# Gated embedding of a two-layer block: four gates by chunk with embedding products between them, table stores moved, tail of the gates interleaved

## What is computed

```python
        h = rmsnorm(x, g_ffn2_pre[i])
        x = x + 0.5 * rmsnorm(swiglu(h, w2_gate[i], w2_up[i], w2_down[i]), g_ffn2_post[i])

        h = rmsnorm(x, g_ple_pre[i])
        e = jax.nn.sigmoid(h @ w_ple_gate[i]) * (p[i].astype(x.dtype) @ w_ple_proj[i])
        x = x + rmsnorm(e, g_ple_post[i])
```

## Time and profile before

| | us |
|---|---|
| median of three runs | 3695.54 |
| their lowest and highest | 3688.07, 3698.82 |
| the profiled execution, its own time | 3689.66 |
| its span, first to last instruction | 3688.4 |
| PE busy in the span | 3459.0 (94%) |
| POOL busy | 2418.4 (66%) |
| DVE busy | 1802.9 (49%) |

### The profile page before, as it was taken

The page is one execution under the profiler, slowest core; times in us unless marked ns, Lnnn a source line. Parts: engine busy times, 40 slices in busy tenths (PEclk is TensorE's granted clock), DMA queues, the critical chain, the costliest instruction groups (busy, mean ns, idle before and its releaser), DMA issues. The chain is left out here.

```text
span 3688.4 us, 42456 instructions
## 1 busy us (share of the span) xinstructions
PE 3459.0 (94%) x15371; PEld 2698.8 (73%) x15384; DVE 1802.9 (49%) x1934; ACT 719.3 (20%) x1404; POOL 2418.4 (66%) x1113
## 2 busy tenths in 40 slices
PE   7999998899998999999899998986999999779998
PEld 6888765688876888775678886654788877558886
DVE  5452535454647545334464474687454323354521
ACT  2110133311123111103321112214311100231100
POOL 7888741488876887763178886650488777328875
PEclk9999998999998999999899999997999999899999
DMA  3233220122331223221022332220122333102232
GB/s 122 97 100 103 86 69 18 58 95 96 109 120 60 94 95 103 86 91 46 18 88 96 104 104 92 92 69 1 56 94 96 103 104 108 40 26 95 97 100 94
DMA packets 84366, 305.98 MB, mean 83 GB/s; under 512 B 9360, under 2 KB 9616, under 8 KB 83856
## 3 DMA queue, kind: packets, MB, share of 16 engines
q1 hardware_dynamic: 80928, 292.59, 23.7%
q10 hardware_dynamic: 3312, 11.71, 0.8%
HBM read 300.07 MB, written 4.19 MB: 82 GB/s over the span
## 5 line engine op out<-in xcount | busy, mean ns | idle before, releaser
L469 POOL TENSOR_TENSOR WH<-raw,zero 128x1024 fp32r<-128x1024 f32 (+1 forms) x554 | 1045.2, 1887 | 1200.6 <-DMA raw<-in_w 1105.7
L471 POOL TENSOR_TENSOR WL<-raw,WH 128x1024 fp32r<-128x1024 f32 (+1 forms) x554 | 1375.0, 2482 | 43.5
L539 PE MATMUL psA<-HH,WH 128*128 128x512 f32 x1216 | 483.6, 398 | 2.3 <-DVE PROJ L1509 2.3
L540 PE MATMUL psA<-HH,WL 128*128 128x512 f32 x1216 | 474.7, 390 | 0.0
L541 PE MATMUL psA<-HL,WH 128*128 128x512 f32 x1216 | 474.7, 390 | 0.0
L541 PE MATMUL psC<-HIDL,WH 128*128 128x512 f32 x1056 | 417.1, 395 | 0.0
L539 PE MATMUL psC<-HIDH,WH 128*128 128x512 f32 x1056 | 417.1, 395 | 0.0
L540 PE MATMUL psC<-HIDH,WL 128*128 128x512 f32 x1056 | 417.1, 395 | 0.0
L1338 DVE TENSOR_TENSOR HIDL<-Y,HIDH 128x512 f32 (+1 forms) x132 | 257.1, 1948 | 126.7 <-ACT HIDH L1060 126.7
L539 PE MATMUL psC<-HH,WH 128*128 128x512 f32 x800 | 314.0, 392 | 3.8 <-DVE HL L1410 3.8
L541 PE MATMUL psC<-HL,WH 128*128 128x512 f32 x800 | 312.3, 390 | 0.0
(11 more groups left out here) (274 smaller groups left out, 4896.2 us busy)
## 6 DMA issues: line engine op xcount, KB each, us to landing
raw<-in_w SPq DMA_DIRECT2D x554, 512.0 KB, 3.3
X<-in_x ACTq DMA_DIRECT2D x4, 512.0 KB, 8.9
NRAW<-in_mem ACTq DMA_DIRECT2D x2, 1024.0 KB, 5.2
out<-Y SPq DMA_DIRECT2D x8, 256.0 KB, 2.1
POSI<-in_pos ACTq DMA_DIRECT2D x4, 256.0 KB, 3.0
PRAW<-in_p ACTq DMA_DIRECT2D x2, 512.0 KB, 4.5
table_F<-newF ACTq DMA_DIRECT2D x2, 512.0 KB, 5.1
table_I<-newI ACTq DMA_DIRECT2D x2, 512.0 KB, 7.8
```

Source lines behind the costliest of these rows:

```text
L469: pool.tensor_tensor(WH[j][:, 0:w], raw[j][:, 0:w], zero[:, 0:1].broadcast_to([P, w]), ALU.subtract).then_inc(w_hi, 1)
L471: pool.tensor_tensor(WL[j][:, 0:w], raw[j][:, 0:w], WH[j][:, 0:w], ALU.subtract).then_inc(w_split, 1)
L539: pe.matmul(out, WH[slot][:, w], hi[:, t], start=start and t == 0, stop=False)
L540: pe.matmul(out, WL[slot][:, w], hi[:, t], start=False, stop=False)
```

## The change

- **PE.** embed() and project_gates() become embed_and_gates(). The first embedding product stands between the two mean-square matmuls, products 1 to 3 behind them. first_four(), which other stages use with four ring slots, now also takes a list of slots, a wait of its own ahead of the second pair (room) and a function to call behind each chunk (between). Here it makes gates 0 to 3 chunk by chunk, gates 2 and 3 one chunk behind from slots RING and RING + 1, with embedding products 4 to 7 behind chunks 0 to 3. Then come the mean square of X and gates 4 to 7. The banks of gates and products are given out anew.
- **POOL.** At this border RING and RING + 1 are split ahead of the wait for hl_ready.
- **ACT.** The stores of newF and newI are issued behind the fourth sine, four down outputs earlier. The gates' loop is interleaved: sigmoid(m), then the square of m - 1.
- **DVE.** The gates' loop is interleaved: T(m), then Y(m - 1), then the addition of m - 2.

No arithmetic is added or taken away; the weight stream and SP's program are the same.

```diff
-    em_bank = lambda m: (PA, PB)[m // 2 % 2][:, m % 2]
+    em_bank = lambda m: (PA if m < 2 else PB)[:, m % 2]
+    ple_bank = lambda g: (PC, PA, PB, PC)[g // 2][:, g % 2]
...
             ffn()
-            border()
-            rounds(4)
+            ring(RING)
+            split(RING, TILES)
+            split(RING + 1, TILES)
+            pool.wait_ge(hl_ready, n.full(hl_ready, 6))
+            n.full(hl_ready, 2)
+            ring(RING)
...
-        def first_four(outs):
-
-            four = [(next_slot(), out) for out in outs]
+        def first_four(outs, slots=None, room=None, between=None):
+
+            four = list(zip(slots or [next_slot() for _ in outs], outs))
 
             def second_pair(k):
                 if k == 0:
                     pe.wait_ge(w_split, n.full(w_split, 2))
+                    if room is not None:
+                        room()
                 for slot, out in four[2:]:
                     chunk_high(slot, out, k)
                     chunk_low(slot, out, k)
@@ -585,6 +580,8 @@
                 pe.wait_ge(hl_ready, n.full(hl_ready))
                 for slot, out in four[:2]:
                     chunk_low(slot, out, k)
+                if between is not None:
+                    between(k)
             second_pair(KD - 1)
...
+        def embed_and_gates():
+
+            held = (next_slot(), next_slot())
+            made, taken_before = n.now(em_done), n.now(pj_done)
+            n.full(em_done, KD)
+
+            def embed(m):
+                if m >= 4:
+                    pe.wait_ge(em_done, made + m - 1)
+                piece(held[m // 4], em_bank(m), PH, PL, 2, first_tile=2 * (m % 4), done=piece_used if m % 4 == 3 else part_done)
+
+            pe.wait_ge(yss_step, n.full(yss_step, KD - 2))
+            pe.matmul(MS_Y, onen, YSS[:], start=True, stop=False)
             pe.wait_ge(p_ready, n.full(p_ready, 2))
...
+            pe.wait_ge(w_split, n.full(w_split, 2))
+            embed(0)
+            pe.wait_ge(ysq_ready, n.full(ysq_ready, KD))
+            pe.matmul(MS_Y, onen, SQ[:, 1], start=False, stop=True).then_inc(ms_ready, 1)
+            for m in range(1, 4):
+                embed(m)
+            first_four([ple_bank(g) for g in range(4)], [next_slot(), next_slot(), RING, RING + 1],
+                       lambda: pe.wait_ge(em_done, made + 2), lambda k: embed(4 + k) if k < 4 else None)
+            mean_square_x()
+            pe.wait_ge(em_done, n.now(em_done))
+            for g in range(4, KD):
+                if g >= 6:
+                    pe.wait_ge(pj_done, taken_before + g - 5)
+                whole(ple_bank(g))
+            n.room(pj_done, KD)
...
-            if layer is not None:
-                act.wait_ge(tab_ok, n.now(tab_ok))
-                for k, tab in (("F", newF), ("I", newI)):
-                    load(saved[k], tab[:], tab_saved)
...
                     if m == 2 * len(tabs) - 1:
                         tables_for(LOG_EXP)
+                        if len(tabs) > 1:
+                            act.wait_ge(tab_ok, n.now(tab_ok))
+                            for k, tab in zip("FI", tabs):
+                                load(saved[k], tab[:], tab_saved)
...
-            for m in range(KD):
-                dve.wait_ge(piece_used, n.full(piece_used))
-                dve.nop(nofuse=True)
-                dve.tensor_tensor(T[:, m % 2], PC[:, m] if m < 2 else PA[:, m % 2], RS[:], ALU.mult).then_inc(pj_done, 1)
-                n.full(pj_done)
-                if m >= 2:
-                    add_squares(m - 1)
-                dve.wait_ge(sg_ready, n.full(sg_ready))
-                dve.nop(nofuse=True)
-                dve.tensor_tensor(Y[:, m], T[:, m % 2], PROJ[:, m], ALU.mult).then_inc(yb_ready, 1)
+            for m in range(KD + 1):
+                if m < KD:
+                    dve.wait_ge(piece_used, n.full(piece_used))
+                    if m >= 2:
+                        dve.wait_ge(yb_ready, n.now(yb_ready))
+                    dve.nop(nofuse=True)
+                    dve.tensor_tensor(T[:, m % 2], ple_bank(m), RS[:], ALU.mult).then_inc(pj_done, 1)
+                    n.full(pj_done)
+                if m > 0:
+                    dve.wait_ge(sg_ready, n.full(sg_ready))
+                    dve.nop(nofuse=True)
+                    dve.tensor_tensor(Y[:, m - 1], T[:, (m - 1) % 2], PROJ[:, m - 1], ALU.mult).then_inc(yb_ready, 1)
+                    n.full(yb_ready)
+                if m >= 3:
+                    add_squares(m - 2)
```

More of the change, by code:

```diff
@@ L553, in chunk_low @@
                 mm.then_inc(piece_used, 1)
-        def first_pair(outs):
-            pair = [(next_slot(), out) for out in outs]
-            pe.wait_ge(w_split, n.full(w_split, 2))
-            for k in range(KD):
-                pe.wait_ge(hh_ready, n.full(hh_ready))
-                for slot, out in pair:
-                    chunk_high(slot, out, k)
-                pe.wait_ge(hl_ready, n.full(hl_ready))
-                for slot, out in pair:
-                    chunk_low(slot, out, k)
-        def first_four(outs):
-            four = [(next_slot(), out) for out in outs]
+        def first_four(outs, slots=None, room=None, between=None):
+            four = list(zip(slots or [next_slot() for _ in outs], outs))
             def second_pair(k):
@@ L642, in ffn @@
                         piece(next_slot(), PC[:, m % 2], HIDH[:, 8 * q:], HIDL[:, 8 * q:], tiles, q == 0, q == 2)
-            if normed:
+            if normed and not embedding:
                 mean_square_y()
-            if embedding:
-                embed()
-        def embed():
-            pe.wait_ge(p_ready, n.full(p_ready, 2))
-            for m in range(KD):
-                if m % 4 == 0:
-                    slot = next_slot()
-                    pe.wait_ge(w_split, n.full(w_split))
-                if m >= 4:
-                    pe.wait_ge(em_done, n.full(em_done))
-                piece(slot, em_bank(m), PH, PL, 2, first_tile=2 * (m % 4), done=piece_used if m % 4 == 3 else part_done)
-            n.full(em_done, 4)
+        def embed_and_gates():
[8 more added lines that the diff above has]
+            pe.matmul(MS_Y, onen, YSS[:], start=True, stop=False)
+            pe.wait_ge(p_ready, n.full(p_ready, 2))
+            pe.wait_ge(w_split, n.full(w_split, 2))
[13 more added lines that the diff above has]
+            n.room(pj_done, KD)
         def output_room(normed):
@@ L689, in project_mix @@
                     whole(PA[:, p % 2])
-        def project_gates():
-            first_pair((PC[:, 0], PC[:, 1]))
-            mean_square_x()
-            pe.wait_ge(em_done, n.now(em_done))
-            for g in range(2, KD):
-                if g >= 4:
-                    pe.wait_ge(pj_done, n.now(pj_done) + g - 1)
-                whole(PA[:, g % 2], RING + g - 2 if g < 4 else None)
-            n.room(pj_done, KD)
         def to_tokens(which):
@@ L950, in _ @@
             n.full(x_ready, 2 * KD)
-            project_gates()
+            embed_and_gates()
             mean_square_y()
@@ L1203, in _ @@
             tables_for(ACT.Sigmoid)
-            for m in range(KD):
-                act.wait_ge(pj_done, n.full(pj_done))
-                act.nop(nofuse=True)
-                act.activation(T[:, m % 2], T[:, m % 2], ACT.Sigmoid).then_inc(sg_ready, 1)
-                act.wait_ge(yb_ready, n.full(yb_ready))
-                squares_room(m)
-                act.nop(nofuse=True)
-                act.activation(SQ[:, m % 2], Y[:, m], ACT.Square).then_inc(ysq_ready, 1)
+            for m in range(KD + 1):
+                if m < KD:
+                    act.wait_ge(pj_done, n.full(pj_done))
+                    act.nop(nofuse=True)
+                    act.activation(T[:, m % 2], T[:, m % 2], ACT.Sigmoid).then_inc(sg_ready, 1)
+                if m > 0:
+                    act.wait_ge(yb_ready, n.full(yb_ready))
+                    squares_room(m - 1)
+                    act.nop(nofuse=True)
+                    act.activation(SQ[:, (m - 1) % 2], Y[:, m - 1], ACT.Square).then_inc(ysq_ready, 1)
             tables_for(LOG_EXP)
```

1 line of the change is left out of this document (removed).

## The result

| | before | after |
|---|---|---|
| median, 20 runs each | 3695.09 | 3702.56 |
| lowest, highest | 3688.07, 3704.62 | 3690.90, 3709.71 |
| the profiled execution, its own time | 3689.66 | 3698.15 |
| its span | 3688.4 | 3696.8 |
| stretch, layer 1 | 79.63 | 83.75 |

The ratio of after to before is 1.002, with a 95% interval of 1.0011 to 1.0029: 7.5 us slower, within 0.3%. The two stretches are 4.1 and 3.6 longer, 7.7 of the 8.4 that the span has grown. In this and all later tables the stretch runs from the first mean-square matmul on YSS to ACT's Ln on psD behind the gates. The start of layer 1's stretch lay anywhere from 1084 to 1093 in the profiled executions, so rows of two kernels are compared from it.

What follows compares the result with a forecast made beforehand. PE was busy 94% of the span, so gains must come from its holes; the tail, bound by DVE waiting for POOL, takes back more. Layers' +3.3 and +2.7 make +6.0: 3695.7 profiled, 3701.5 median, range 3687 to 3714.

Steps and rivals of the forecast that it cites:

- Embedding ahead of the squares: Start of the stretch: six embedding matmuls between the mean-square matmuls start ACT's Ln later, 1.4 us lost.
- Stores and first HH: ACT early in the stretch: its 4.69 wait for the table stores goes; first HH some 6.3 after the start, not 9.0.
- 2.7 gained: First HH on ACT follows DVE's first X at once, at 1092.95 instead of 1095.67, net of the 1.4 lost.
- POOL's fourth split: Before gates 2 and 3: POOL splits four pieces in a row until 1105.0, leaving PE a new hole of 6.7 us.
- Slow clock: PE's matmuls behind the new hole run at the 1.2 GHz level; charged 2.4 us, bounds 0 and 4.8.
- Rival 3: PE's hole leaves the clock alone: -4.8 from the forecast, +1.2, median 3696.7; chance 0.11.
- RS: After X's mean square: RS at 1133.6 against 1126.3, 7.3 later, but with four gates made instead of two.
- the 0.7 that my sum left them: Before X's mean square: DVE's three additions ready at 1130.6, just ahead of PE, through at 1131.3.
- Last gate: Gates 4 to 7 after RS: 96 matmuls, 22.1 us; PE ends at 1154.3, 5.1 earlier than before.
- Tail: Behind RS: one two-SBUF-input DVE operation per POOL instruction; Y6 ends 1163.65, addition 6 1165.95, Ln 1169.5 instead of 1166.27.
- Rival 2: DVE's tail is not held by POOL and PE ends last: stretch 75.1, -9.6 in all, median 3685.9; chance 0.12.
- Rival 1: PE's wait for POOL's fourth split is longer: +4.6 per layer, 9.2 on top of 6.0, median 3710.7; chance 0.15.

Runs made afterwards that it cites:

- the other run: Changed kernel with gates 2 and 3 four chunks behind, tail in PSUM, old tail order, and table stores put back late: 3666.23, ratio 0.9917 to the kernel before.

## Why the prediction was right, point by point

The forecast was +6.0 on the profiled execution and 3701.5 on the median; measured were +8.5 and 3702.56.

- **Embedding ahead of the squares.** Ln at 3.3 after the start, 1.2 later than before, against 1.4. It stands on no path, as the runs with the squares first show.
- **Stores and first HH.** 6.2 after the start, predicted 6.3. I took the price of the early stores as nothing beyond DMA. What I missed is that the first HH, coming sooner, lets PE reach its hole sooner, so that the hole is one piece and the slow clock falls behind it. With the stores late the stretch is 2 shorter: the step "2.7 gained" was no gain, as far as RS goes.
- **POOL's fourth split.** 18.47 after the start, predicted 18.4. The hole was 6.13, predicted 6.7, since PE stood before the second pair 12.4 after the start and not 11.7: gate 1's split let it start 0.4 later than I had it, and the 16 matmuls took 3.9 and not 3.6. That the split itself came on time is in part luck: four HL operations fell among its instructions and not three, but each cost POOL 0.3 to 0.5 (WH 2.35 for 1.89, WL 2.71 for 2.39) and not 0.55.
- **Slow clock.** 14 matmuls in 6.1 us where 3.2 would do, 2.9 lost; predicted 2.4. The run with the stores late, which has the same matmuls at the 2.4 GHz level, gives the same 2.9. Rival 3 is refuted.
- **RS.** 48.2, predicted 47.0. PE was through the first four gates at 45.7, predicted 44.7: 0.5 of it is the clock and 0.1 to 0.2 the split. The rest, 0.4, is the rate: the 104 matmuls behind the hole, which I had at 0.23 each, 23.9, take 24.3 in the run with the stores late, at the 2.4 GHz level. In layer 2 the three additions kept PE waiting for 0.83, in layer 1 they ended just before it; the 0.7 that my sum left them was less than its errors.
- **Last gate.** 68.6, predicted 67.7, the same 1 us.
- **Tail.** DVE's Y6 ended at 77.8 (predicted 77.0), add6 at 79.9 (79.3), Ln at 83.8 (82.9). POOL's six pieces took 29.8, and the sum has 29.9 for them (1133.2, when the first is loaded, to 1163.1); they began 47.4 after the start and not 46.6, which is the lateness of PE again. The mechanism is shown from both sides by the runs with POOL resting and with PSUM operands. PE's closing matmuls took 3.9 to Ln, with 3.5 predicted. Rival 2, a tail that is not held, is what those two runs look like: stretches of 76.
- **Rival 1**, a later fourth split, did not come, but half of its condition did: two of the three pieces took 5.1. The load of the first was on time, though (POOL waited 0.15), and that piece took 4.4, so the three took 14.5, as in the sum (14.6), and not 15.4.

The largest mis-sized term is the slow clock, 2.4 for 2.9. RS came 1.2 late in all; the tail, which POOL times, gave some of it back (0.6 late at its last addition), and the closing matmuls added 0.3: 83.8 for 82.9. Of the span's growth 0.7 lies outside the stretches and is not explained.

## What to carry to other kernels

When a stage with many weight splits runs beside a vector tail, count the vector operations with two SBUF inputs and give each one whole GpSimd instruction; keeping one operand in PSUM takes the operation off that count, and here it cost no instruction. When chunks are taken by an engine that waits for several weights at once, let the second group lag by as many chunks as its weights are late. And an earlier start somewhere is worth only what the next wait leaves of it; look which hole grows, and where the slow clock behind it will fall.

## What the runs showed of the hardware

- A DVE operation of 128x512 with two SBUF inputs that meets POOL's splits ended 0.55 after POOL's instruction in all pairs read; the 128x2048 addition of the changed kernel, 4.48 long, ended 2.15 after it. The 0.55 holds for products, additions and for HL's three-operand form (2.86 instead of 0.75). POOL's own WH rises from 1.89 to 2.35 and its WL from 2.40 to 2.73 when DVE takes turns with it.
- PE's clock was at the 1.2 GHz level behind one hole of 6.13, and equally behind two holes of 2.42 and 0.79 (2.46 and 0.83 in the other run) with 1.2 us of matmuls between them. It stayed at the 2.4 GHz level behind a hole of 1.07 (first matmul 0.49), and behind the 2.42 and 2.46 until the second hole (first matmul 0.50). Behind the 1.82, which ended a slow stretch, it was back at that level (0.50). The closing mean-square matmul took 2.07 behind holes of 3.37 and 3.54, and 1.12 behind 1.45. The slow stretches among the gates lasted 5 to 6 us.
- I had not expected that here a wait cut in pieces cost less than one in a single piece: the slow clock was paid behind the first holes, while the last one was still ahead.
